# First attention blocks: where block 0's second value group stands among the row-maxima products of blocks 1 and 2

## The reference

```
q = rope(rmsnorm(p[..., Q0:K0], q_g)); k = rope(rmsnorm(p[..., K0:V0], k_g)); v = p[..., V0:GA0]
s = einsum('bqkgd,bskd->bkgqs', q * HEAD_DIM ** -0.5, concat(k, k_ctx))
p = softmax(s, axis=-1)
attn = einsum('bkgqs,bskd->bqkgd', p, concat(v, v_ctx))     # 8 query heads, 2 key heads, head width 64
y = concatenate([attn * silu(ga), fourier_mix(fu, w_f) * silu(gf)]) @ w_o
out = rmsnorm(x + gate * y, final_g)
```

## Time and profile before

| what | value |
| --- | --- |
| median of three runs | 1409.7 us (1409.53 to 1410.79) |
| the profiled execution, its own time | 1412.48 us |
| its span, first to last instruction | 1410.7 us |
| granted TensorE clock, mean | 0.989 |
| PE busy | 1362.8 us, 97% of the span |
| DVE / ACT / POOL busy | 865.1 / 575.4 / 615.8 us |

### The profile page before, as it was taken

How to read it: one execution, slowest core, us unless ns; L and a number is a source line. 1 busy time by engine, 2 the same in 40 slices (tenths; PEclk the granted TensorE clock), 3 DMA queues, 4 the chain that set the end, 5 groups by cost and what they waited for, 6 DMA issues and landing times.

```text
span 1410.7 us, 22314 instructions
## 1 busy us (share of the span) xinstructions
PE 1362.8 (97%) x7878; PEld 926.1 (66%) x7878; DVE 865.1 (61%) x1263; ACT 575.4 (41%) x1061; POOL 615.8 (44%) x309
## 2 busy tenths in 40 slices
PE   6888999999999999999999999999999999999997
PEld 4677785555555555555555554888887888778886
DVE  3677677778777777777777778412322721755452
ACT  3454334545555455545454547232322323522120
POOL 0334115988888889888888883100000000000000
PEclk9999999999999999999999999999999999999999
DMA  9656429011101110111010100922511151785651
GB/s 365 232 151 211 121 67 259 23 38 34 33 26 37 30 37 27 39 30 37 26 37 30 30 26 21 301 79 105 177 47 38 35 226 53 203 210 178 195 154 75
DMA packets 84341, 142.63 MB, mean 101 GB/s; under 512 B 7085, under 2 KB 54325, under 8 KB 83386
## 3 DMA queue, kind: packets, MB, share of 16 engines
q1 hardware_dynamic: 76890, 129.09, 29.0%
q0 software_dynamic: 6672, 12.58, 3.2%
q10 hardware_dynamic: 720, 0.15, 0.1%
HBM read 112.30 MB, written 29.50 MB: 101 GB/s over the span
## 4 chain that ended last, share of the span: by engine, by line
PE 85%; issue 2%; DMA 2%; DVE 1%; ACT 1%; SPq 1%; POOLq 0%; POOL 0%; DVEq 0%
PE pv_ps L1574 18%; PE ring_ps L1558 10%; PE ring_ps L1559 9%; PE acc L63 7%; PE acc L64 7%; PE acc L65 7%; PE ring_ps L1502 6%; PE o_ps L63 4%; PE o_ps L65 4%; PE o_ps L64 4%; PE q_ps L63 1%; PE ring_ps L1582 1%; DMA gin<-rest_scratch 1%; PE q_ps L64 1%; PE q_ps L65 1%
## 5 line engine op out<-in xcount | busy, mean ns | idle before, releaser
L1284 POOL TENSOR_TENSOR prob_sum<-prob_sum,prob 128x1024 f32<-128x1024 f32 x217 | 526.9, 2428 | 86.7 <-DVE prob_sum L1409 63.7
L1388 DVE TENSOR_REDUCE chunk_max<-ring_ps 128x1 f32<-128x512 f32 x496 | 307.7, 682 | 88.2 <-PE ring_ps L1502 87.0
L1323 ACT ACTIVATE prob<-ring_ps 128x512 f32<-128x512 f32 x576 | 290.5, 633 | 72.1 <-PE ring_ps L1559 71.9
L1574 PE MATMUL pv_ps<-prob,v 128*32 128x512 f32 x2304 | 262.1, 598 | 0.0
L1558 PE MATMUL ring_ps<-blk_q_hilo,k_hi 128*128 128x512 f32 x576 | 235.4, 409 | 3.9 <-ACT prob L1323 1.8
L1559 PE MATMUL ring_ps<-blk_q_negm,k_lo 68*128 68x512 f32 x576 | 228.8, 397 | 0.0
L1574 PEld LDWEIGHTS pv_ps<-prob,v 128*32 128x32 f32 x2304 | 68.4, 110 | 151.1 <-issue 135.3
L63 PE MATMUL acc<-hh,w_rest_hi 128*128 128x512 f32 x384 | 151.1, 394 | 0.5 <-DVE hl L98 0.5
L64 PE MATMUL acc<-hl,w_rest_hi 128*128 128x512 f32 x384 | 150.4, 392 | 0.0
L65 PE MATMUL acc<-hh,w_rest_lo 128*128 128x512 f32 x384 | 150.3, 391 | 0.0
L1558 PEld LDWEIGHTS ring_ps<-blk_q_hilo,k_hi 128*128 128x128 f32 x576 | 110.1, 191 | 53.0 <-DVE blk_q_negm L1170 13.8
(11 more groups left out here) (315 smaller groups left out, 1956.6 us busy)
## 6 DMA issues: line engine op xcount, KB each, us to landing
xt_raw<-in_xt SPq DMA_DIRECT2D x16, 512.0 KB, 5.2
x_tok<-in_x SPq DMA_DIRECT2D x16, 512.0 KB, 4.9
blk_q_max<-q_scratch SPq DMA_DIRECT2D x64, 128.0 KB, 2.6
blk_q_hilo<-q_scratch SPq DMA_DIRECT2D x32, 256.0 KB, 2.7
h_raw<-in_xg SPq DMA_DIRECT2D x4, 2048.0 KB, 9.2
rest_scratch<-stage SPq DMA_DIRECT2D x32, 256.0 KB, 2.3
gin<-rest_scratch SPq DMA_DIRECT2D x16, 512.0 KB, 10.8
x_res<-in_x SPq DMA_DIRECT2D x16, 512.0 KB, 3.4
```

Source lines behind the costliest of these rows:

```text
L1284: nc.gpsimd.tensor_tensor(acc_pool[slot][:], acc_pool[slot][:], prob[j][:], ALU.add).then_inc(s_psum, 1)
L1323: nc.scalar.activation(prob[j][:, e * QB:(e + 1) * QB], score_bank(t)[:], ACT.Exp).then_inc(s_exp, 1)
L1388: nc.vector.reduce_max(chunk_max[:, q, c:c + 1], ring[banks[c]][:], X_AXIS).then_inc(s_mfree, 1)
L1574: last = nc.tensor.matmul(pv_ps[row:row + QUAD], k.v[:, 2 * j + e, kvh, half * QUAD:(half + 1) * QUAD], prob[j][:, e * QB:(e + 1) * QB], s ...
```

## The change

It is made in PE's instruction order alone, and in two places. No instruction is added or taken away, and no wait of any other engine is edited.

```
@@ value_products
                 for j in range(*GROUP_PAIRS[group]):
-                    if j == 3 and isinstance(b, int) and b == 0:
+                    if j == 2 and isinstance(b, int) and b == 0:
                         max_chunks(1, 1, kvh, 2)
@@ first_body
                 value_products(0, 0, 0, 0)
                 max_chunks(1, 1, 0, 3)
                 max_context(1, 1, 0)
-                value_products(0, 0, 0, 1)
                 k.turn_max(pe, row_ps, 1, lambda: exp_done(0, KT - 1))
                 pe.wait_ge(s_qm[0], 64)
                 max_chunks(2, 0, 0, 0)
                 first_scores(1, 1, 0, True)
                 max_chunks(2, 0, 0, 1)
+                value_products(0, 0, 0, 1)
                 max_chunks(2, 0, 0, 2)
```

## The result

The changed kernel took 1413.83 us, median of 22 runs (1409.06 to 1420.41), the kernel before 1409.01 us beside it. The ratio is 1.0033, 95% interval 1.0022 to 1.0043: 4.65 us slower, 3.1 to 6.1. The time lies above the range, and the kernel is slower.

What follows compares the result with a forecast made beforehand. PE, busy for 97% of the span, was taken to bound the kernel. The terms 1.38 - 1.55 + 1.2 = +1.0 us on 1409.7 gave 1410.7 us, range 1409.0 to 1412.9.

Steps and rivals of the forecast that it cites:

- Steps 1 and 2: Block 1's third set of maxima one pair earlier: cost 0 to 0.1 us, taken 0; DVE gains 0, at most 0.1.
- Step 3: Value group 1 leaves its place ahead of block 1's turning: PE idles 3.4 to 3.6 us there, 0 us on the path.
- Step 4: Value group 1 between sets 1 and 2 of block 2's maxima: set 1 to second scores costs +1.38 us.
- Step 5: Slow clock at 256.8 us, over block 1's second scores, goes away: -1.55 us.
- Step 6: New slow clock behind the idle stretch, from turning into block 1's first scores: +1.2 us, bounds 0 and 3.1.
- rival D: Clock stays low for a second stretch behind the idle one: up to 3.1 us, 1412.6 to 1414.2 us; chance 0.09.
- Step 7: Other engines' work that moves, such as block 0's evacuate, combine, fold and store: cost 0, at most 0.3 us.
- B: Clock stays up behind the idle stretch ahead of block 1's turning: 1409.5 us; chance 0.12.
- C: Timed runs lack the slow clock of 256.8 us, so removing it returns nothing: +2.6 us, 1412.3 us; chance 0.15.
- E: A later short lull, such as at 870 us, changes sides: 1.5 us either way, 1409.2 or 1412.2 us; chance 0.12.

Runs made afterwards that it cites:

- filled kernels: Changed kernel plus 14 or 7 unread matmuls in PE's idle stretch ahead of the turning; ratio to before 1.0007 and 1.0000 with 14, 1.0000 with 7.
- split version: Kernel before with only pairs 7 and 8 of block 0's value group 1 moved between block 2's maxima sets 1 and 2; ratio to before 0.9988.
- three score tiles: Kernel before with block 1's first three second-score tiles put ahead of set 2 of block 2's maxima; ratio to before 0.9986 and 0.9991.

## Why the prediction was wrong, step by step

**Steps 1 and 2** held. The third set cost 0.1 us, DVE got nothing from it, the negated maximum came as early as before (turning 9.81 us after the first value matmul, against 9.72).

**Step 3** held: 3.5 us of idle, where 3.4 to 3.6 was said, released by DVE.

**Step 4** held: +1.36 us in the first trace for 1.38 forecast.

**Step 5** held in the traces: -1.54 us for -1.55. That the slow clock belongs to each execution of before wasn't shown beyond its three traces, and neither the times nor the clocks of the timed runs settle it.

**Step 6** failed, by its size. It priced the slow clock behind the new idle stretch at one stretch of 3.4 us, +1.2 us. The clock stayed low for 6.8 us, in all five traces that have this idle stretch, and it cost 0.52 + 2.26 = 2.78 us. That the clock falls about when PE wakes was right, but the forecast's count (3.4 us behind the beginning of the idle stretch) fits only the first trace, where it fell at 245.4 and the idle stretch began at 241.9: over the five traces it fell 2.8 to 4.3 us behind that beginning, so the exact agreement is luck. I had taken the duration from the row at 130.5 to 133.8 and from before's own at 256.8, one stretch each, and kept the double one as rival D at 0.09. With 2.78 in it the sum is 0.09 + 1.36 - 1.54 + 2.78 = 2.69 us, 1412.4. That is D's mechanism, just under its lower edge of 1412.6, and what the traces and two of three comparisons of the changed kernel show. It still lies inside the forecast's range: step 6 accounts for 1.6 us of the miss, and the further 2 us of the first comparison stay open (below). D's reason, thin work behind the waking, wasn't shown. PE was busy for all of 6.40 us of the slow stretch in the first trace, and the kernel with only the third set moved had the double stretch with scores alone behind its lull.

**Step 7** held: the delay stays constant from block 1 to the last block.

Of the rivals, B (clock stays up) is what the filled kernels look like, C is without support in any trace but not excluded for the timed runs, and E wasn't needed: later slow stretches, such as that near 873, stand in traces of both kernels.

**What stays open.** The first comparison says 4.65 us (3.1 to 6.1), the traces 2.4 to 2.8. The mean granted clock of the 22 executions of after was 0.9869, against 0.9892 of the 12 on the last chip, which is 6.5 us more at the lower level over a span of 1412, worth about 3 us at half pace. So those executions had more slow clock than the others, but whether the change had a hand in that can't be said, because only one of them has a trace. Why the slow stretch behind a full idle one is double isn't settled either: the kernel with only the third set moved had the double one behind a lull in which before had the single one three times.

The page "TensorE: Matmul & The Clock Gate" of the Trainium skill, section "Why this matters for your kernels", whose rule on idle gaps the forecast had weighed, was right in kind: the gap brought the lower clock, 0.50, in all five traces. Its section on the clock gate says that the switching isn't tied to the kernel's start. The five onsets agree in that they don't keep one place against the work either: they lie 0.7, 0.4, 0.3 and 0.1 us before PE's waking and 0.8 us behind it.

## What to carry to other kernels

When work is moved on TensorE, price the place it leaves as well as the place it goes to: leaving a stretch empty in which another engine's chain has to be waited for anyway delays nothing by itself, but an idle TensorE of 3.5 us cost 2.8 us more through the clock, while 1.6 and 1.7 us (one trace each) left the clock up. Two short lulls were cheaper than one long one (the split version, 23.21 against 27.46 us for the stretch). And look for work that uses other banks than the ones being waited for, as the three score tiles did, before moving work out of a place where it covers something. Where a forecast has seen a slow stretch of one length in a single trace, it should price up to twice that length.

## What the runs showed of the hardware that I had not expected

Behind these lulls the lower clock lasted 3.4 or 6.8 us. TensorE was busy through nearly all of the longer ones (6.50 of 6.50 us busy at 0.50 in the kernel with only the third set moved), so work alone didn't bring the clock back at once. Matmuls whose result nobody reads, on real data, kept it up: 14 of them took 2.8 us out of the stretch, and 7 did the same. And single executions of one kernel on one chip differ by some 10 us, more than any effect here. Part of it comes before the attention's first values: over all traces but that of 2220.53 us, in programs that are alike up to there, block 0's first value matmul started between 233.2 and 239.4 us.
